# Full 128x128 stationary tiles for head sums and gate rows, and the three products of an attention step in one group

## The reference, cut to what matters

```python
# first block: 8 query heads and 2 key heads of 128, normed per head, then rotated
q = rms_norm(q.reshape(B, L, 8, 128), q_g);  k = rms_norm(k.reshape(B, L, 2, 128), k_g)
s = einsum('btkgd,blkd->bkgtl', q, k) * 128 ** -0.5     # 256 latent rows, 512 keys
p = softmax(s);  o = einsum('bkgtl,blkd->btkgd', p, v)
# even layer: gates of 4 heads, one number per token and head
b = cumsum(fc);  Dm = where(tri, b_t - b_s + ic_s, -1e30);  m_t = maximum(m_inter, max(Dm))
W = exp(Dm - m_t);  Sc = (q k^T) * W;  h = num / maximum(abs(den), exp(-m_t))
```

## Time and profile before

| what | value |
|---|---|
| three runs | 1361.89, 1363.85, 1367.06 us |
| median | 1363.85 us |
| profiled execution, its own time | 1367.78 us |
| its span, first to last instruction | 1365.3 us |
| TensorE matmul busy | 1323.2 us (97%) |
| TensorE weight load busy | 1214.3 us (89%) |
| DVE, ACT, POOL busy | 906.4, 648.5, 30.3 us |
| mean granted TensorE clock | 0.987 of full |
| DMA, mean | 168 GB/s |

### The profile page before, as it was taken

How to read it: one execution, slowest core, us unless ns; L and a number is a source line. 1 busy time by engine, 2 the same in 40 slices (tenths; PEclk the granted TensorE clock), 3 DMA queues, 4 the chain that set the end, 5 groups by cost and what they waited for, 6 DMA issues and landing times.

```text
span 1365.3 us, 23443 instructions
## 1 busy us (share of the span) xinstructions
PE 1323.2 (97%) x9310; PEld 1214.3 (89%) x9310; DVE 906.4 (66%) x1462; ACT 648.5 (48%) x1025; POOL 30.3 (2%) x29
## 2 busy tenths in 40 slices
PE   5999999999999999999999999999999999999996
PEld 3688888888898889899999999989999999998996
DVE  3577875546558486654775555788886757688853
ACT  3433222223236335554554444666666766555552
POOL 0000000000010000000000000200000001000000
PEclk6999999999999999999999999999999999999998
DMA  8755656555544344444556565556544554355550
GB/s 301 259 168 185 213 195 209 172 199 203 173 134 157 106 124 150 142 140 155 175 155 189 183 192 169 158 163 182 162 148 140 173 167 156 112 161 180 183 168 31
DMA packets 201403, 229.67 MB, mean 168 GB/s; under 512 B 7120, under 2 KB 191696, under 8 KB 201296
## 3 DMA queue, kind: packets, MB, share of 16 engines
q1 hardware_dynamic: 201008, 227.90, 52.7%
q10 hardware_dynamic: 288, 0.29, 0.1%
HBM read 227.11 MB, written 1.05 MB: 167 GB/s over the span
## 4 chain that ended last, share of the span: by engine, by line
PE 85%; DVE 9%; ACT 3%; issue 2%; DMA 1%; SPq 0%; DVEq 0%; ACTq 0%
PE P L1030 25%; PE P L1031 25%; PE P L1032 25%; DVE WL L1855 2%; DVE TS L1783 1%; PE P L1146 1%; PE P L1036 1%; PE P L1038 1%; PE P L1037 1%; PE P L1134 1%; PE P L992 1%; DMA W<-in_w_mod 1%; ACT WH L1450 1%; PE P L1123 1%; PE P L1139 1%
## 5 line engine op out<-in xcount | busy, mean ns | idle before, releaser
L1030 PE MATMUL P<-XHB,WH 128*128 128x256 f32 (+1 forms) x1808 | 562.1, 311 | 11.1 <-DVE TS L1822 4.0
L1031 PE MATMUL P<-XLB,WH 128*128 128x256 f32 (+1 forms) x1808 | 546.6, 302 | 0.0
L1032 PE MATMUL P<-XHB,WL 128*128 128x256 f32 (+1 forms) x1808 | 546.4, 302 | 0.0
L1855 DVE TENSOR_TENSOR WL<-W,WH 128x1024 fp32r<-128x1024 f32 x358 | 431.5, 1223 | 103.7 <-ACT WH L1450 103.4
L1450 ACT ACTIVATE WH<-W 128x1024 fp32r<-128x1024 f32 x358 | 369.0, 1041 | 258.0 <-PE P L1032 180.2
L1030 PEld LDWEIGHTS P<-XHB,WH 128*128 128x128 f32 x1808 | 341.3, 189 | 39.1 <-issue 18.4
L1031 PEld LDWEIGHTS P<-XLB,WH 128*128 128x128 f32 x1808 | 341.2, 189 | 17.9 <-issue 3.1
L1032 PEld LDWEIGHTS P<-XHB,WL 128*128 128x128 f32 x1808 | 343.0, 190 | 14.9
L1030 PE MATMUL P<-GH,WH 128*128 128x256 f32 (+1 forms) x372 | 122.0, 328 | 0.0
L1031 PE MATMUL P<-GL,WH 128*128 128x256 f32 (+1 forms) x372 | 121.5, 326 | 0.0
L1032 PE MATMUL P<-GH,WL 128*128 128x256 f32 (+1 forms) x372 | 121.5, 326 | 0.0
(11 more groups left out here) (302 smaller groups left out, 1814.3 us busy)
## 6 DMA issues: line engine op xcount, KB each, us to landing
W<-in_ffn_w_in SPq DMA_DIRECT2D x88, 512.0 KB, 4.7
W<-in_w_in_ab SPq DMA_DIRECT2D x72, 512.0 KB, 4.5
W<-in_w_modt SPq DMA_DIRECT2D x56, 512.0 KB, 3.9
W<-in_w_in SPq DMA_DIRECT2D x52, 512.0 KB, 3.6
W<-in_ffn_w_out SPq DMA_DIRECT2D x40, 512.0 KB, 4.6
W<-in_w_in_c SPq DMA_DIRECT2D x32, 512.0 KB, 4.1
W<-in_w_mod SPq DMA_DIRECT2D x16, 512.0 KB, 6.9
W<-in_w_out_ab SPq DMA_DIRECT2D x16, 512.0 KB, 4.4
```

The source lines that it names most:

```text
L1030: pe.matmul(o, h[:, k, c], xh[:, kk, a:b], start=kk == 0, stop=False)
L1031: pe.matmul(o, h[:, k, c], xl[:, kk, a:b], start=False, stop=False)
L1032: mm = pe.matmul(o, l[:, k, c], xh[:, kk, a:b], start=False, stop=kk == gm.nk - 1)
L1855: dve.tensor_tensor(l, a, h.bitcast(F32), ALU.subtract).then_inc(S["wl"], 1)
```

## The change

It has four parts.

1. `qa` uses 128x128 stationary tiles. `HOT` is a strip of 131 columns, zero but for column 3, that lies in `MC` (unused until later); a window of 128 columns of it puts the sum of head `i` into row `i` and zeros into all others. POOL fills it at its start, after DVE's 56th product for the modulation, and TensorE waits for it. Root and reciprocal are taken over all 128 rows.
2. `qb` and `m0` use `sel` with all 128 rows. `G` now has 128 partitions; POOL clears the two rows of it that are spread, between two of its sums, and DVE waits for that in `g2`.
3. `qk_norm` sets the rotation of a head directly ahead of the next head's `qb`, with two yields after each.
4. `attention` sets `score(i + 1)`, the gather and `turn(i)` side by side, and ACT's exponentials become a step of their own, `exp`, behind them.

```diff
-for _name, _n in (("id", 128), ("one", 128), ("eps", 1), ("ee", 1), ("hot", 16), ("gat", 2), ("cnt", 26), ("perm", 128),
+for _name, _n in (("id", 128), ("one", 128), ("eps", 1), ("ee", 1), ("gat", 2), ("cnt", 26), ("perm", 128),
...
     def qk_norm(self, s):
         for i in range(4):
+            if todo is not None:
+                self.rope(*todo)
+                todo = None
             b, f = self.bank(self.up("qn"))
             self.step("qb", a=s, b=i, c=self.at("qn"), bank=b, free=f)
-            at = self.at("qn")
-            yield
-            if todo is not None:
-                self.rope(*todo)
-                yield
-                todo = None
             if s < 2 or i % 2:
-                todo = (s, i, at)
+                todo = (s, i, self.at("qn"))
             else:
                 self.ready.add(self.name(s, i))
-                self.end[self.name(s, i)] = at
+                self.end[self.name(s, i)] = self.at("qn")
+            yield
+            yield
...
     def attention(self):
         score(0)
+        self.step("exp", a=0, bank=4 + (self.uses - 1) % 3)
         for i in range(16):
-            yield
-            yield
+            for _ in range(2):
+                yield
             self.step("scale", a=i)
+            for _ in range(2):
+                yield
             if i + 1 < 16:
                 while missing(i + 1):
                     yield True
                 score(i + 1)
-            yield
+                bank = 4 + (self.uses - 1) % 3
             if i and i % 2 == 0:
                 b, f = self.bank(self.up("ol"))
                 self.step("gather", a=i // 2 - 1, bank=b, free=f)
-            yield
             b, f = self.bank(self.up("at"))
             self.step("turn", a=i, bank=b, free=f)
-        for _ in range(3):
+            if i + 1 < 16:
+                self.step("exp", a=i + 1, bank=bank)
+        for _ in range(2):
             yield
...
+        HOT = MC[:, 0, 0:131]
-            G = sbuf(st, "G", [4, 6, T])
+            G = sbuf(st, "G", [128, 6, T])
-            return MC[0:4, 7, :] if s == 2 else RS[0:4, 1, T * s:T * s + T]
+            return MC[:, 7, :] if s == 2 else RS[:, 1, T * s:T * s + T]
...
                 elif s.kind == "qa":
+                    pe.wait_ge(S["hot"], 2)
-                        pe.matmul(ps[0:4, 0:T], con("hot", 4 * i, 4 * i + 4), SQ[:, n % 3, T * (n // 3 % 2):T * (n // 3 % 2) + T], start=i == 0,
+                        pe.matmul(ps[:, 0:T], HOT[:, 3 - i:131 - i], SQ[:, n % 3, T * (n // 3 % 2):T * (n // 3 % 2) + T], start=i == 0,
                 elif s.kind == "qb":
-                    pe.matmul(ps[:, 0:T], con("sel", 128 * s.b, 128 * s.b + 128, 4),
+                    pe.matmul(ps[:, 0:T], con("sel", 128 * s.b, 128 * s.b + 128),
                 elif s.kind == "m0":
-                    pe.matmul(ps[:, 0:T], con("sel", 128 * h, 128 * h + 128, 4), G[:, 4, 0:T], start=True, stop=True)
-                    pe.matmul(ps[:, T:2 * T], con("sel", 128 * h, 128 * h + 128, 4), G[:, 5, 0:T], start=True,
+                    pe.matmul(ps[:, 0:T], con("sel", 128 * h, 128 * h + 128), G[:, 4, 0:T], start=True, stop=True)
+                    pe.matmul(ps[:, T:2 * T], con("sel", 128 * h, 128 * h + 128), G[:, 5, 0:T], start=True,
...
         def _(pool):
+            pool.wait_ge(S["md"], 56)
+            pool.memset(HOT, 0.0).then_inc(S["hot"], 1)
+            pool.wait_ge(S["hot"], 1)
+            pool.memset(HOT[:, 3:4], 1.0).then_inc(S["hot"], 1)
             for name in ("s2", "s3", "s4", "s5", "s7"):
...
+                if name == "s3":
+                    pool.wait_ge(S["oh"], 8)
+                    pool.memset(G[:, 4:6, :], 0.0).then_inc(S["gz"], 1)
...
-                elif s.kind == "score":
+                elif s.kind == "exp":
...
+                    dve.wait_ge(S["gz"], 1)
                     dve.tensor_scalar(neg, top, -1.0, None, ALU.mult).then_inc(S["dv"], 1)
```

More of the change, by code:

```diff
@@ L78, in constants @@
     put("ee", np.full((128, 1), EPS * EPS, np.float32))
[L79 to L82, removed]
     put("gat", (p[:, None] % 32 == np.arange(2)[None, :]).astype(np.float32))
@@ L838, in build_program @@
         seq, stat, end = plan.seq, plan.stat, plan.end
-        names = ("g wh wl zero sc mm mr mt mv md cb sf sq pa on sr ra ri rb am gm out sil1 hm1 hh1 hl1 xu1 sil2 hm2 hh2 hl2 xu2 "
+        names = ("g wh wl zero gz hot sc mm mr mt mv md cb sf sq pa on sr ra ri rb am gm out sil1 hm1 hh1 hl1 xu1 sil2 hm2 hh2 hl2 xu2 "
                  "nt nh nl xh xr rx "
@@ L1166, in _ @@
                     for j in range(2):
-                        mm = pe.transpose(ps[:, 4 * j:4 * j + 4], G[:, 2, 128 * j:128 + 128 * j], con("id", 0, 4, 4))
+                        mm = pe.transpose(ps[:, 4 * j:4 * j + 4], G[0:4, 2, 128 * j:128 + 128 * j], con("id", 0, 4, 4))
                     mm.then_inc(S["gmm"], 1)
@@ L1534, in _ @@
                     act.wait_ge(S["qh"], 4 * s.a + 4)
-                    act.activation(rows_of(s.a), ps[0:4, 0:T], ACT.Sqrt, scale=1.0 / 128, bias=con("eps", rows=4)) \
+                    act.activation(rows_of(s.a), ps[:, 0:T], ACT.Sqrt, scale=1.0 / 128, bias=con("eps")) \
                         .then_inc(S["qr"], 1)
-                elif s.kind == "score":
+                elif s.kind == "exp":
                     i = s.a
@@ L1554, in _ @@
                 elif s.kind == "g1":
-                    t2 = G[:, 2, 0:T]
+                    t2 = G[0:4, 2, 0:T]
                     act.wait_ge(S["gfree"], 1)
-                    act.activation(t2, G[:, 1, 0:T], ACT.Abs).then_inc(S["gab"], 1)
+                    act.activation(t2, G[0:4, 1, 0:T], ACT.Abs).then_inc(S["gab"], 1)
                     act.wait_ge(S["gab"], 1)
@@ L2057, in _ @@
                     dve.wait_ge(S["gr0"], 1)
-                    dve.tensor_scalar(G[:, 0, 0:T], TS[0:4, 5, 0:T], V[0:4, VEC["bi"][0]:VEC["bi"][1]], None, ALU.add) \
+                    dve.tensor_scalar(G[0:4, 0, 0:T], TS[0:4, 5, 0:T], V[0:4, VEC["bi"][0]:VEC["bi"][1]], None, ALU.add) \
                         .then_inc(S["gr0"], 1)
@@ L2061, in _ @@
                     dve.wait_ge(S["gmm"], 1)
-                    dve.tensor_scalar(G[:, 1, 0:T], ps[0:4, T:2 * T], V[0:4, VEC["bf"][0]:VEC["bf"][1]], None, ALU.add) \
+                    dve.tensor_scalar(G[0:4, 1, 0:T], ps[0:4, T:2 * T], V[0:4, VEC["bf"][0]:VEC["bf"][1]], None, ALU.add) \
                         .then_inc(S["gfree"], 1)
                 elif s.kind == "g2":
-                    ig, b, t2, top, neg = (G[:, i, 0:T] for i in range(5))
+                    ig, b, t2, top, neg = (G[0:4, i, 0:T] for i in range(5))
                     dve.wait_ge(S["gfree"], 1)
@@ L2082, in _ @@
                     dve.wait_ge(S["dv"], own)
-                    dve.tensor_tensor(G[:, 5, 0:T], neg, b, ALU.subtract).then_inc(S["gq"], 1)
+                    dve.tensor_tensor(G[0:4, 5, 0:T], neg, b, ALU.subtract).then_inc(S["gq"], 1)
                 elif s.kind == "g4":
```

## The result

| | before | after |
|---|---|---|
| median of 12 runs of each on one chip | 1365.56 us | 1353.82 us |
| lowest and highest | 1359.34, 1369.56 | 1351.40, 1362.06 |
| ratio, 95% interval | | 0.9928 [0.9908, 0.9948] |
| profiled execution, its own time | 1367.78 us | 1355.05 us |
| its span | 1365.3 us | 1353.0 us |

Faster by 0.72% [0.52%, 0.92%], some 9.8 us of 1363.85; forecast were 7.6. A second measurement of the same two kernels (at the end of the experiments) gave only 0.46%. So the mean holds a part that isn't the change's alone, and the question was which.

A forecast was written before the change was run, and what follows sets the result against it. TensorE's stream of issued matmuls was taken as the bound. Terms 4.6 + 0.9 + 1.1 + 0.3 + 0.7 = 7.6 us bring the median from 1363.85 to 1356.2 us; 8 in 10 range 1351.0 to 1362.9.

The forecast's parts named there:

- `qb`, 4.6 us: Spreading a head's row, 12 times: full 128-row tiles cost 0.44 us instead of 0.82, saving 4.6 us.
- `qa`, 0.9 us: Head sums, 3 times: full tiles cost 1.73 us like the gather instead of 2.03, saving 0.9 us.
- `m0`, 1.1 us: Gate rows, 4 times: full tiles save 0.35 us for three heads and 0.1 for the first, 1.1 us.
- Joining, 0.3 us: Side products in `attention` and `qk_norm` set together: 30 breaks fewer at 0.01 us each, saving 0.3 us.
- The turn's wait, 0.7 us: In `attention`, a turn's wait for DVE's scaled exponentials and one smaller wait go, saving 0.7 us.
- I take zero: Chunk matmuls' step of 0.113 or 0.118 us: unforecastable, counted as zero, up to 3.7 us either way per stage.
- Theory A: Experiments' theory: the sum's terms are real, as sized, additive; the swiglu's 6.8 us are a step set by chance, then kept.
- B: Experiments' theory: joining does more than 0.01 us a break, since a group ending in turns sets the step short.
- C: Experiments' theory: the second swiglu's shorter step, 6.8 us, is the change's doing too.
- as summed: Rival for the whole kernel: steps of both lengths mixed as now, 1353.5 to 1359 us; chance 0.47.
- the short step prevails: Rival: chunk matmuls take the short step in one stage or both, about 1352 us; chance 0.14.
- D: Gaps at `qb` come from the operands, not the tile's form; as the prediction's rival, 1362.9 us, chance 0.08.

The follow-up runs named there:

- e5: The kernel before with each `qb` matmul issued twice, the second overwriting the first; one run 1364.49 us, kernel before 1359.96 us.
- e6: The changed kernel with 64 rows in `qb` and 64 columns in `qa`; one run 1364.11 us, kernel before 1359.96 us.
- e3: The changed kernel with turn, gather, score as the order inside each group; median 1357.22 us, ratio to the kernel before 0.9934.
- e2: The kernel before with the new `qk_norm`, `attention` and `exp`, narrow tiles kept; median 1355.18 us, ratio to the kernel before 0.9915.
- e1: The changed kernel with the old `qk_norm`, `attention` and place of the exponentials; median 1355.41 us, ratio to the kernel before 0.9935.
- e12: The changed kernel once more, unaltered, beside the kernel before on another chip; median 1358.60 us, ratio 0.9954.

## Why the prediction was right or wrong

**The bound**: right. TensorE's stream is the time; no wait came, and what was taken from the stream was taken from q to ma.

**`qb`, 4.6 us**: right in size (4.63), in place (the start 0.12 behind the matmul ahead) and in cause. That a rotation of the same columns is what a `qb` in the full form would cost was the right neighbour, and e5 and e6 show the reason: entering and leaving the narrow form, paid with 4 rows and with 64.

**`qa`, 0.9 us**: right (0.87). The gather was the right row for the weight loads too; laid bare they never were.

**`m0`, 1.1 us**: a little low, 1.25. I took 0.35 a head from the gaps of single records; start to start over the whole group it was 0.38.

**Joining, 0.3 us**: too much, 0.13. A break between full tiles is worth 0.003 to 0.007 us, not 0.01.

**The turn's wait, 0.7 us**: right (0.83 with the smaller one). "No turn waits for ACT" held, and e3 shows what the position at the end of the group was worth: with the turn first, 1.6 us of waits.

**At no cost** (POOL's addition, root and reciprocal, the memsets): right, by the rows and times of POOL and ACT above.

**"I take zero"**: this is the step that failed. The prediction set the step of the chunk matmuls to zero in the sum and bounded it by 3.7 us for each of two stages, those with changed steps. Two things were wrong with it. Behind groups that end in turns the step was not a matter of chance: 15 of 15 short, and e2 shows 2.3 us of steps won from q to ma by the order alone. The wide tiles alone lost 0.6 (e1), and 1.4 is what both together won. And the largest piece lies in the second swiglu, which the prediction had named as the place where nothing should move: the earlier trace rows show that the step there held through 1361 matmuls, and from "it holds" should have followed "what sets it at the start decides on 1578 of them, 6.8 us". The forecast's own sign of being wrong, time that moves from 700 to 860 us, therefore came true, for this term.

In sum: forecast terms 7.6, measured 7.7. The profiled executions' 12.3 us (1365.3 to 1353.0) are these 7.7, 1.4 of step in q to ma, 6.8 in the swiglu and 0.6 ahead of `q`, less 4.2 that came back from the even layer on. By runs it is 9.8 us at first and 6.3 us (0.46% of 1363.85) in e12, where the changed kernel had the low times less often. That the whole came so near to 7.6 is in part luck: the pieces of the steps, each up to 6.8 us, have both signs and were not forecast. Theory A stands for the terms, but not for "by chance", and B for some 2 us of the order, with a wrong reason; of C, e5 and e6 leave this: no part of the change is needed for a short swiglu, nor is it enough; whether the change shifts how often the swiglu falls short was neither shown nor excluded. The rival "as summed" (1353.5 to 1359) holds both measurements, 1353.8 and 0.9954 times 1363.85, 1357.6; the first lies at the edge of "the short step prevails". D, the rival that the narrow tile is not what costs, is out. What sets the step behind an interruption was not found.

## What to carry to other kernels

Where TensorE is the bound, read the distance between starts, not busy time: a lone product with 4 or with 64 rows cost its columns plus 0.38 us for going into the narrow form and out of it. Pad it with zeros to 128 rows, or put all narrow products next to each other, as the second one in a row paid nothing extra. Joining full products gave next to nothing by itself (0.13 us for 28 breaks); order them so that the one that waits for another engine comes last.

And before explaining a gain of under 1%, tabulate the time stage by stage: here 6.8 of the profiles' 12.3 us lay in a stage that the change doesn't touch, and the stage with the change added up to 0.15 us and came out again within 0.5 us whenever a kernel was profiled twice, while ratios of whole runs had the two parts sum to twice the change.

## What the runs showed that I had not expected

- The distance of back-to-back chunk matmuls has two values, 0.113 and 0.117 us, at the same granted clock of 1.00. It can change at each side product and is then kept for as long as nothing interrupts, 1482 matmuls and more. It is worth 6.8 us in one stage, nearly as much as the whole change.
- An identical group of a 512-column product and four transposes left it long in two kernels and short in two others (three executions). From q to ma the changed kernel, profiled twice, had the same step behind all 34 groups.
- 64 rows pay as much as 4 for the narrow form, 96 nothing.
- Weight loads that went from 87 to 190 ns cost nothing when hidden under the four products of `qa`, which got 0.29 us cheaper.
